# Four row slots instead of five, with the memory's keys and values kept on chip between portions 0 and 1

## The reference

```
u,v,val,gate,q,gl_a,gl_b,gl_m = split(rmsnorm(x) @ w_in)
A = gelu(u) * (tril(W_s) layernorm(gelu(v)) + b)      # chunks of 128
B = silu(layernorm(causal_conv31(val * sigmoid(gate))))
M = attention(q, k, v)      # prompt: k, v = rmsnorm(mem) @ w_mem_k, w_mem_v; sample: cached k, v
x = x + W_out(sig(gl_a)*A W_oA + sig(gl_b)*B W_oB + sig(gl_m)*M W_oM)
per token, 8 heads: the 16 best of 16384 experts by product keys
x = x + sum_k softmax_k * gelu(xn . U[e_k]) * V[e_k]
```

## Time and profile before

| | before |
|---|---|
| median of 3 runs | 2285.98 us |
| profiled execution: span, first to last instruction | 2288.1 us |
| its time as a run (the profile gives only the span; the nearest run) | 2288.86 us |
| TensorE / VectorE / ScalarE / GpSimd busy | 72% / 69% / 29% / 29% |
| mean granted TensorE clock | 0.796 |
| moved by DMA | 898.68 MB, 393 GB/s over the span |
| share of the 16 DMA engines' span: gathers / SP's queue | 63.9% / 32.1% |

### The profile page before, as it was taken

One profiled execution on the slowest core, in us unless ns is written; L12 is line 12 of the kernel. 1 busy time (PEld: TensorE's weight loads), 2 busy tenths in 40 slices (PEclk: granted clock), 3 DMA queues, 4 the chain that ended last, 5 costly groups with the idle time before them and its releaser, 6 DMA issues.

```text
span 2288.1 us, 31202 instructions
## 1 busy us (share of the span) xinstructions
PE 1641.2 (72%) x10876; PEld 1065.3 (47%) x10876; DVE 1576.5 (69%) x4199; ACT 662.5 (29%) x1662; POOL 669.6 (29%) x596
## 2 busy tenths in 40 slices
PE   8999977669997657788878746865999853334333
PEld 8865766337885335454433414642887620000001
DVE  3545277779766666877675657976875777776875
ACT  2112234231232332323123223342123233332222
POOL 0000032222332532323213333321322354444442
PEclk9999989779997768889889756977989875555555
DMA  8686689999999999999999999999999999999997
GB/s 297 264 291 242 259 360 422 419 421 414 412 421 414 416 421 421 421 406 414 421 391 415 421 421 418 419 401 411 411 385 421 405 403 421 422 421 422 421 421 303
DMA packets 127675, 898.68 MB, mean 393 GB/s; under 512 B 16128, under 2 KB 16960, under 8 KB 19488
## 3 DMA queue, kind: packets, MB, share of 16 engines
q0 software_dynamic: 83232, 604.02, 63.9%
q1 hardware_dynamic: 44288, 292.68, 32.1%
HBM read 888.53 MB, written 8.11 MB: 392 GB/s over the span
## 4 chain that ended last, share of the span: by engine, by line
PE 36%; DMA 34%; DVE 18%; issue 4%; ACT 4%; DVEq 3%; POOL 2%; another core or an unknown queue 0%; POOLq 0%; SPq 0%; ACTq 0%
DMA uv<-uv_in,idx_u 25%; PE bank L1475 16%; DVE uv L1354 8%; DMA ring<-w_in 7%; PE bank L1481 5%; PE bank L1981 5%; PE bank L1730 5%; DVE yB L940 2%; DMA ring<-cache_in 2%; POOL uv L482 1%; ACT diag L857 1%; ACT L534 1%; DVEq L935 1%; DVE x L1375 1%; PE bank L1488 1%
## 5 line engine op out<-in xcount | busy, mean ns | idle before, releaser
L482 POOL DMA_INDIRECT uv<-uv_in,idx_u x574 | 654.0, 1139 | 1393.7 <-PE bank L1981 1068.0
L1354 DVE CUSTOM_DVE_ANT_0 uv<-uv,xrep 128x1024 f32<-128x1024 f32 x576 | 681.9, 1222 | 202.2 <-DMA uv<-uv_in,idx_u 190.6
L1981 PE MATMUL bank<-uv,diag 128*32 128x512 f32 x2176 | 399.8, 816 | 460.3 <-ACT diag L857 455.0
L1475 PEld LDWEIGHTS bank<-xnT,ring 128*128 128x128 f32 x3200 | 443.5, 204 | 81.7 <-issue 69.5
L1475 PE MATMUL bank<-xnT,ring 128*128 128x160 f32 (+1 forms) x3200 | 465.3, 307 | 6.1 <-DMA ring<-w_in 4.7
L534 ACT ACTIVATE pick<-pick 128x2 f32<-128x2 f32 (+1 forms) x324 | 69.6, 215 | 1049.7 <-DVE pick L1354 1047.6
L1981 PEld LDWEIGHTS bank<-uv,diag 128*32 128x32 f32 x2176 | 50.2, 123 | 650.6 <-ACT diag L857 578.0
L940 DVE SCALAR_TENSOR_TENSOR yB<-ext_p,small,yB 128x128 f32<-128x128 f32 x960 | 278.2, 352 | 20.4 <-issue 1.1
L534 ACT ACT_TABLE_LOAD x140 | 179.6, 1283 | 2.5
L857 ACT ACTIVATE diag<-gated_fold,pick 128x32 f32<-128x32 f32 x576 | 153.6, 314 | 9.6 <-ACT pick L534 0.2
L1730 PE MATMUL bank<-ring,xnT 128*128 128x512 f32 x192 | 89.0, 619 | 0.0
(11 more groups left out here) (224 smaller groups left out, 1766.9 us busy)
## 6 DMA issues: line engine op xcount, KB each, us to landing
ring<-w_in SPq DMA_DIRECT2D x220, 1024.0 KB
ring<-cache_in SPq DMA_DIRECT2D x32, 1024.0 KB
uv<-uv_in,idx_u POOLq DMA_INDIRECT x578, 12.9
uv<-w_in SPq DMA_DIRECT2D x4, 1024.0 KB, 14.0
ext_s<-state_in SPq DMA_DIRECT2D x2, 1088.0 KB, 10.7
convs_out<-ext_s SPq DMA_DIRECT2D x2, 1088.0 KB
ext_s<-mem_in SPq DMA_DIRECT2D x2, 1024.0 KB, 19.8
memk_out<-phase SPq DMA_DIRECT2D x2, 1024.0 KB, 12.1
```

The costliest lines, as they stand in the source:

```text
L482: nc.gpsimd.indirect_dma_start(out=uvbuf[2 * b + i], out_offset=None, in_=uv_in, in_offset=bass.IndirectOffsetOnAxis(ap=ids[:, c:c + 1], a ...
L1354: ins = V.tensor_tensor_reduce(out=u, in0=u, in1=xrep[gg % 2][:, :], scale=1.0, scalar=0.0, op0=ALU.mult, op1=ALU.add, accum_out=hid[:, c: ...
L1475: ins = MM(out, w[:, k, P * b:P * (b + 1)], rhs(k), start=k == 0, stop=k == KB - 1)
L1981: ins = MM(vbank[gg % 2][c:c + 32, :], diag[:, t % 4, i], uvbuf[2 * b + i][:, D + 512 * n:D + 512 * (n + 1)], start=first, stop=last)
```

## The change

`SLOTS` goes from 5 to 4, so that `uv` has 8 buffers. The room of the two that go (16 KB per partition) becomes two tensors of their own, `kT` and `vmem`, which nothing else overwrites before the next layer. The loads at L406 and L430 go, with the waits ahead of them on SP and the waits for their landing on TensorE. The waits that protected `phase` go or are replaced: ScalarE's for the scores and the store of the keys ahead of `va` 0, SP's for `pe_o` and `v_stored` ahead of `wsT`. In layer 1 the first writes of `kT` and `vmem` wait for layer 0's stores. The early weights move to buffers 4 to 7, the sample rows to buffer 3, and the waits of the first gathers move one gather ahead.

```diff
-SLOTS = 5
+SLOTS = 4
-        xr_first = [xrep[1][:, :], uvbuf[5][0:T_S, 0:D]]
-        kT = phase[:, 0:2 * D].rearrange("p (c t) -> p c t", c=KB)
-        vmem = phase[:, 2 * D:4 * D].rearrange("p (m d) -> p m d", m=2)
+        xr_first = [xrep[1][:, :], uvbuf[3][0:T_S, 0:D]]
+        kT_flat, vmem_flat = sb("kT", [P, 2 * D])[:, :], sb("vmem", [P, 2 * D])[:, :]
+        kT = kT_flat.rearrange("p (c t) -> p c t", c=KB)
+        vmem = vmem_flat.rearrange("p (m d) -> p m d", m=2)
...
-                    if p == 1 and n == 8:
-
-                        sp.wait_ge(S["pe_xt"], at("pe_xt", m, 3))
-                        sp.wait_ge(S["pe_sc"], at("pe_sc", m, 0))
-                        sp.wait_ge(k_stored, 16 * (l + 1))
-                        sp.dma_start(phase[:, 0:2 * D], memk_out[rows_l, :]).then_inc(k_landed, 16)
...
-                    if p == 0 and (kind, i) == ("out", 0):
-
-                        sp.wait_ge(S["pe_sgu"], at("pe_sgu", m + 1, 0))
-                        sp.dma_start(phase[:, 2 * D:4 * D], memv_out[rows_l, :]).then_inc(v_landed, 16)
                     if (kind, i) == (("mg", 2), ("ck", 5))[p]:
-                        sp.wait_ge(S["pe_o"], at("pe_o", m, 4))
-                        sp.wait_ge(v_stored, 16 * (l + 1))
+                        sp.wait_ge(S["pe_sgu"], at("pe_sgu", m, 0))
...
-                if t == 2:
+                if t == 1:
                     pool.wait_ge(S["pe_xt"], at("pe_xt", 1, 3))
-                if t in (3, 4):
-                    pool.wait_ge(S["pe_glu"], at("pe_glu", 1, 4 * (t - 2)))
+                if t in (2, 3):
+                    pool.wait_ge(S["pe_glu"], at("pe_glu", 1, 4 * (t - 1)))
                 if t >= SLOTS:
                     pool.wait_ge(S["v_used"], t - SLOTS + 1)
...
-                        act.wait_ge(S["pe_xt"], at("pe_xt", m, 2))
+                        if m:
+                            act.wait_ge(k_stored, 16 * l)
...
+                    if m and i == 0:
+                        act.wait_ge(v_stored, 16 * l)
...
-                    if i == 0:
-
-                        act.wait_ge(S["pe_s"], at("pe_s", m, 4))
-                        if p == 0:
-                            act.wait_ge(k_stored, 16 * (l + 1))
...
-                    if p:
-                        pe.wait_ge(k_landed, 16 * (l + 1))
-                    else:
+                    if p == 0:
                         pe.wait_ge(S["kt"], at("kt", m, h + 1))
```

More of the change, by code:

```diff
@@ L221, in build @@
         mem_landed, state_landed, ws_landed = sem("mem_landed"), sem("state_landed"), sem("ws_landed")
-        k_stored, v_stored, k_landed, v_landed = sem("k_stored"), sem("v_stored"), sem("k_landed"), sem("v_landed")
+        k_stored, v_stored, = sem("k_stored"), sem("v_stored")
         fing_landed, y_rows = sem("fing_landed"), sem("y_rows")
@@ L354, in buf @@
             if (m, kind, i) in EARLY:
-                return uvbuf[6 + i]
+                return uvbuf[4 + i]
             return ring[ITEM[m, kind, i] % RING]
@@ L415, in _ @@
                         sp.wait_ge(S["kt"], at("kt", m, 4))
-                        sp.dma_start(memk_out[rows_l, :], phase[:, 0:2 * D]).then_inc(k_stored, 16)
+                        sp.dma_start(memk_out[rows_l, :], kT_flat).then_inc(k_stored, 16)
                     if p == 0 and (kind, i) == ("va", 3):
                         sp.wait_ge(S["vm"], at("vm", m, 4))
-                        sp.dma_start(memv_out[rows_l, :], phase[:, 2 * D:4 * D]).then_inc(v_stored, 16)
+                        sp.dma_start(memv_out[rows_l, :], vmem_flat).then_inc(v_stored, 16)
                     if m == 0 and (kind, i) == ("mv", 0):
@@ L425, in _ @@
                             r = WROW["glu", c]
-                            sp.dma_start(uvbuf[6 + c], w_in[P * r:P * (r + 1), :]).then_inc(early_landed[c], 16)
-                    if p == 0 and (kind, i) == ("out", 0):
-                        sp.wait_ge(S["pe_sgu"], at("pe_sgu", m + 1, 0))
-                        sp.dma_start(phase[:, 2 * D:4 * D], memv_out[rows_l, :]).then_inc(v_landed, 16)
+                            sp.dma_start(uvbuf[4 + c], w_in[P * r:P * (r + 1), :]).then_inc(early_landed[c], 16)
                     if (kind, i) == (("mg", 2), ("ck", 5))[p]:
-                        sp.wait_ge(S["pe_o"], at("pe_o", m, 4))
-                        sp.wait_ge(v_stored, 16 * (l + 1))
+                        sp.wait_ge(S["pe_sgu"], at("pe_sgu", m, 0))
                         sp.dma_start(wsT, ws_in[rows_l, :].rearrange("p (g t) -> p g t", g=KB)).then_inc(ws_landed, 16)
@@ L1594, in att_out @@
                     pe.wait_ge(S["pt"], at("pt", m, h + 1))
-                    if p:
-                        pe.wait_ge(v_landed, 16 * (l + 1))
-                    else:
+                    if p == 0:
                         pe.wait_ge(S["vm"], at("vm", m, h + 1))
```

## The result

The changed kernel takes 2295.05 us (median of 6 runs, 2289.42 to 2298.53) against 2288.89 us (6 runs, 2285.95 to 2290.94): a ratio of 1.0023, 95% interval 1.0012 to 1.0034, or +2.7 to +7.8 us, +5.3 in the middle. It is slower, as forecast, but by little: 5.3 us lie just outside the 4.6 us (0.2%) that the forecast called no change, and the interval reaches into them. The forecast said +22.4 us, and its range of 2278 to 2332 us holds the time only because it was wide. The profiled execution spans 2293.8 us, 5.7 more than that of before, and took 2295.49 us as a run.

The account below looks back on a forecast made before the run. The prediction took DMA transfer at 421 GB/s from about 300 us on as the bound. Adding 29.9 us for the lost slot and subtracting 7.5 for removed bytes gave +22.4, 2308.4 us; 8-in-10 range 2278 to 2332.

Parts of the forecast that it names:

- first kind: Stretches such as 780 to 960 us where work waits for gathers; in the second kind (1600 to 1860 us) transfers run ahead.
- ten places: Dips of the DMA rate below 421 GB/s, 315 to 2250 us: seven lose 3.5 us each, three 1.8, 29.9 in all.
- three reloads: Removed key and value loads where DMA engines are full: 2.49 us each, 7.5 us gained; the first value load counted nothing.
- a byte less is worth its transfer time: From about 300 us to the end, removed bytes gain their transfer time at 421 GB/s, 2.49 us per 1 MB load.
- Pure expert stretches: Four slots cost nothing there: 13.4 us remain for a gather's flight against 10.9 measured; 1900 to 2000 us stays at 421 GB/s.
- Rival C: Four slots short everywhere: cycle 5.48 us per pair for 4.98, 42 us over the last 85 pairs, about 2350 us; chance 0.11.
- named places: The ten dips of the DMA rate, where the rate was to fall further, with new stretches below 400 GB/s beside them.
- mild one near 735: One of the ten dips, at 735 us, among the three priced at 1.8 us.
- VectorE's waits for gathers: Sign: these waits grow from 190.6 us, above all just after mixing stretches.
- gathers of pairs 2 and 3: Start of the experts: issued near 311 and 321 us, pair 3 up to 5.9 us late; not added to the sum.
- Rival B: A draw: the ten dips cost about 0.75 us each, 7.5 in all, and the time stays at 2286.0 us; chance 0.10.

Follow-up runs that it names:

- h1: Kernel before, five slots, eight weight loads of portion 3's mixing (1600 to 1850 us) cut to an eighth, part of the result left out: 1.0010.
- e1: Kernel before with gathers into four slots only, the fifth's room unused and the reloads kept: 1.0030, +6.9 us.
- the six: Traces with one pair less queued in the mixing: the change, e1, e2, e4, g1 and j1; measured ratios 1.0020 to 1.0041.
- f3: e1 with eight extra 1 MB loads in the pure expert stretch, after pairs 233 to 268: 1.0111 against the kernel before, 18.5 us over e1.
- g1: Kernel before with four slots, six weight ring buffers in place of four, reloads kept, first gathers later: 1.0030.
- e4: The changed kernel again, unedited, beside the other experiments, against the kernel before: 1.0030, +6.9 us.
- e2: Changed kernel with the two reloads per layer put back at their old places and waits, against the kernel before: 1.0041, +9.4 us.
- j1: Kernel before, five buffers, gathers queued four pairs ahead up to pair 207 (mixing), five from there on: 1.0020, +4.6 us.
- e3: Kernel before, five slots, four reloads removed, a constant tile replacing keys and values in the attention of portions 1 and 3: 0.9996, -0.9 us.
- h2: Kernel before with eight loads of portion 2's first weights (issued 785 to 900 us) cut to an eighth, part of the result left out: 0.9922, -17.9 us.
- f4: e1 with eight extra 1 MB loads beside portion 3's gate weights in the mixing: 1.0104 against the kernel before, 17.0 us over e1.
- f1: Kernel before, five buffers, gathers queued only three pairs ahead up to pair 207 (mixing), five from there on: 1.0323, +74 us.
- f2: Kernel before, five buffers, gathers queued five pairs ahead up to pair 207, three from there on (experts only): 1.0215, +49 us.

## Why the prediction was wrong in size

**The failed step** is the sentence that "a microsecond in which the DMA engines have nothing left to do is a microsecond lost at the next stretch of the first kind", and with it the count of ten places at 1.8 to 3.5 us. A full DMA share in a stretch with mixing does not say that transfers set the pace. They run ahead there until slots and ring are full, at whatever rate they can, and h1 shows that their rate can fall to 186 GB/s at no cost. What is carried into the next stretch is then not the transfers done but the lead: at most the slots and the ring. One slot less makes that lead one pair shorter, once for each entry into a stretch that the gathers pace. Three entries show it (near 770, 1250 and 1860 us), at 2.2 to 5.5 us each. In e1 they sum to 13.8 us, in the change to 9.9. My term had about the right price and the wrong number of places. That the steps lie there is read from seven traces (the six and f3's, whose extra loads begin later); that a shorter lead makes them is argued from where they lie and from their size. The entry near 1045 us, which costs next to nothing, and the second slot, whose 67 us are far above three more pairs' transfer, show that this count is a rule of thumb for the first slot only.

**What is given back.** Between pairs 156 and 168 (1465 to 1585 us) the six traces win 3.8 to 9.9 us, 6.2 on average. Taken from the average sum of the steps, 11.4 us, this leaves 5.3, near the measured 5 to 7; for single traces the sum is rougher (2.7 in the change, 8.2 in e1). The forecast had nothing of this, and it had two of its ten losses here, where the dips vanish. In that stretch TensorE waits for weights. Its waits there before (the first line), with four slots only, and after the change:

```profile
PEld bank L1481 <- DMA ring<-w_in: 15.5, 2, 12.0
```

```profile
PEld bank L1482 <- DMA ring<-w_in: 10.8, 2, 9.3
```

```profile
PEld bank L1469 <- DMA ring<-w_in: 3.9, 2, 2.7
```

That a shorter queue of gathers lets the weights land sooner fits these lines, and the other traces too: where the wait is 2.7 to 4.7 us (g1, the change, e4) the gain is 5.9 to 9.9, where it is 10.8 to 13.4 (e1, e2, j1) it is 3.8 to 5.6, and e3 has 14.1 and 2.2. No run tests it by itself, and the keys' reload at 1428 us, which is gone in the change and in e4, plays into it. The cause stays open.

**The bytes.** I took 7.5 us for three reloads and measured 0.9 (e3) to 2.5: about one. The traces name it. The value reload of layer 1 (issued at 1232.79 us, just before a gather-paced stretch) gains 3.0 us in e3 (pairs 120 to 144, -3.9 to -6.9), and over the same pairs the change and e4 stand at -0.4 each, where e1, e2, g1 and j1 with their reloads lose 2.0 to 3.7. The two reloads of keys (301 and 1428 us) stand ahead of mixing stretches and show no such gain with five slots: e3 loses 1.0 us from pair 0 to 48 and wins 2.2 at the place just discussed. So "a byte less is worth its transfer time" holds in the first kind of stretch (h2) and not in the second (h1).

**The sign of added bytes.** f4 and h1 are the same eight loads in the same place, added and taken away, and they measure +17 and about +2 us. The base of f4 has four slots and that of h1 five, so they are not a perfect mirror. Yet 17 us on one side and nothing on the other fit a stretch in which TensorE's chain and the transfers are about equally long, so that the kernel sits at the bend: more bytes cost and fewer do not help. Eight loads more into five slots would test it; that was not run, nor was a sixth slot. f1 shows the bend for the slots, 7 us for the first and 67 for the second.

**What held.** Pure expert stretches keep the 421 GB/s of the earlier trace rows with four slots, and from pair 204 to 287 the change loses 1.2 us, the other four with four slots there 0.1 to 3.0. Rival C is out, with some 80 pairs at 0.00 to 0.04 us each in place of 0.5. The rates in the named places fell further in all but those at 1500 and 1560 us (the mild one near 735 moved to 720). VectorE's waits for gathers grew, as forecast. The gathers of pairs 2 and 3 were issued where forecast, in these lines of the changed kernel:

```profile
306.56 1.12 POOL L472 DMA_INDIRECT uv<-uv_in,idx_u  x1 [13.04 <-PE bank L1463]
...
316.45 0.94 POOL L472 DMA_INDIRECT uv<-uv_in,idx_u  x1 [7.53 <-PE bank L1463]
```

They come 4.7 us earlier than in the earlier trace rows, in an execution that began its experts 4.2 us earlier. Rival B's size (a quarter of the price per dip) is nearest to the slot's measured 7 us, but not its mechanism of a small loss at each dip, and its draw needed the bytes to be worth 7.5, which they are not. On the Trainium skill's advice ("Trainium Kernel Development and Optimization", Best Practices, double buffering) f2 gives a measure for this kernel: three pairs ahead are too few even where nothing but gathers runs, by 0.61 us a pair.

## What to carry to other kernels

A full DMA queue is a bound only where somebody waits for what it brings. Before a price is put on a lost byte or buffer, look in each stretch for who waits for landings, and count the entries from stretches paced by compute into stretches paced by transfers: in this kernel the first buffer's lead was spent at three of four such entries, once each, and not at every dip of the rate. Do not carry the price over to a second buffer: here it cost ten times the first. To see on which side of the bend a stretch lies, add some loads and cut some: here two such runs told what the DMA share did not.

## What the runs showed of the hardware

Single executions of one kernel differ more than the effects looked for: the four profiled executions of e1 to e4 span 2301.9, 2290.1, 2281.3 and 2288.3 us, where their medians are 2294.2, 2296.2, 2287.5 and 2293.2. Much of the difference between traces arises in portion 0, before the experts (first product at 295.0 to 303.4 us). A difference of 5.7 us between two profiled spans was the right size here by luck.
